# x in two column halves with the identity alone first, and the split of b_e1 behind the first residual additions, in a one-core hybrid attention and expert block

## What is computed

```python
h = rmsnorm(x, g_mix);  z = h @ w_in                     # 1024 x 5184, in column chunks
o_a, o_b = nsa_mixer(...), dsa_mixer(...)                # two sparse attentions
merged = sigmoid(ga) * (o_a @ w_branch_a) + sigmoid(gb) * (o_b @ w_branch_b)
x = x + merged @ w_out                                   # the first residual addition
x = x + moe_ffn(rmsnorm(x, g_ffn), w_router, b_router, w_e1, b_e1, w_e2, b_e2)
x = x + sigmoid(rmsnorm(x, g_ple) @ w_ple_gate) * (p @ w_ple)

# moe_ffn: the top 4 of 32 experts by router logits; for each chosen (token, expert):
gu = xe @ w1[e] + b1[e]
act = (clip(gu[:, F:], -7, 7) + 1) * min(gu[:, :F], 7) * sigmoid(1.702 * min(gu[:, :F], 7))
y += weight * (act @ w2[e] + b2[e])
```

## Time and profile before

| | us |
|---|---|
| median of 3 runs (lowest, highest) | 1254.29 (1253.6, 1255.81) |
| the profiled execution, its time | 1253.69 |
| its span in the profile | 1251.6 |
| TensorE busy | 1147.2 (92%) |
| VectorE busy | 273.8 (22%) |
| ScalarE busy | 188.6 (15%) |
| DMA queue of SyncE | 441.45 MB, 85.0% of 16 engines' span |
| chain that ended last | PE 58%, DMA 38%, ACT 2%, DVE 1% |

### The profile page before, as it was taken

One profiled execution on the slowest core, in us unless ns is written; L12 is line 12 of the kernel. 1 busy time (PEld: TensorE's weight loads), 2 busy tenths in 40 slices (PEclk: granted clock), 3 DMA queues, 4 the chain that ended last, 5 costly groups with the idle time before them and its releaser, 6 DMA issues.

```text
span 1251.6 us, 15209 instructions
## 1 busy us (share of the span) xinstructions
PE 1147.2 (92%) x6372; PEld 477.0 (38%) x6372; DVE 273.8 (22%) x786; ACT 188.6 (15%) x405; POOL 34.8 (3%) x49
## 2 busy tenths in 40 slices
PE   7999999988999999998899888888888888888878
PEld 4455544434433334333333333333333333333334
DVE  1473534243211112111111111111111111111122
ACT  2223434222111111111110000000000000000010
POOL 2121100000000000000000000000000000000000
PEclk9999999988999999999999999999999999999999
DMA  8935050966999999999999999999999999999980
GB/s 281 321 135 187 15 135 1 398 231 261 428 426 428 429 427 428 428 429 429 424 427 428 429 428 428 428 428 429 429 430 428 428 428 427 429 429 429 427 344 34
DMA packets 51209, 448.29 MB, mean 358 GB/s; under 512 B 9265, under 2 KB 11926, under 8 KB 26502
## 3 DMA queue, kind: packets, MB, share of 16 engines
q1 hardware_dynamic: 49582, 441.45, 85.0%
q0 software_dynamic: 1264, 5.27, 1.2%
q10 hardware_dynamic: 328, 1.08, 0.3%
HBM read 446.71 MB, written 4.22 MB: 360 GB/s over the span
## 4 chain that ended last, share of the span: by engine, by line
PE 58%; DMA 38%; ACT 2%; DVE 1%; issue 0%; ACTq 0%; POOL 0%; DVEq 0%; POOLq 0%
DMA ring<-in_w_e 24%; PE ps L369 16%; DMA wbuf<-in_w_e 12%; PE ps L396 11%; PE ps L1315 7%; PE ps L1397 5%; PE ps L347 3%; PE ps L338 2%; PE ps L1514 2%; PE ps L1428 2%; PE ps L1361 2%; PE ps L1449 1%; DMA oT<-in_b_e 1%; ACT wbuf L460 1%; PE ps L386 1%; PE ps L1388 1%
## 5 line engine op out<-in xcount | busy, mean ns | idle before, releaser
L369 PE MATMUL ps<-ring,wbuf 128*64 128x512 f32 x1392 | 312.1, 595 | 35.0 <-DMA ring<-in_w_e 34.8
L369 PEld LDWEIGHTS ps<-ring,wbuf 128*64 128x64 f32 x1392 | 96.0, 136 | 238.5 <-issue 162.2
L507 DVE TENSOR_SCALAR oT<-ps 128x512 f32<-128x512 f32 x32 | 22.1, 692 | 736.2 <-PE ps L369 736.2
L369 PE MATMUL ps<-wbuf 128*64 128x512 f32 x656 | 147.8, 595 | 17.6 <-DMA wbuf<-in_w_e 17.4
L396 PE MATMUL ps<-ring,wbuf 128*64 128x512 f32 x672 | 149.5, 595 | 14.2 <-ACT wbuf L460 14.2
L456 ACT ACTIVATE oT<-oT 128x512 f32<-128x512 f32 x32 | 20.2, 630 | 509.8 <-DVE oT L507 509.8
L369 PEld LDWEIGHTS ps<-wbuf 128*64 128x64 f32 x656 | 45.2, 136 | 113.4 <-issue 75.4
L1315 PE MATMUL ps<-wbuf,hT 128*128 128x512 f32 (+2 forms) x224 | 85.4, 540 | 1.0 <-ACT hT L705 1.0
L396 PE MATMUL ps<-wbuf 128*64 128x512 f32 x352 | 78.6, 595 | 7.4 <-ACT wbuf L460 7.4
L396 PEld LDWEIGHTS ps<-ring,wbuf 128*64 128x64 f32 x672 | 46.4, 137 | 102.1 <-issue 83.9
L347 PE MATMUL ps<-wbuf 64*128 64x512 f32 x264 | 65.6, 615 | 0.7 <-ACT wbuf L462 0.7
(11 more groups left out here) (237 smaller groups left out, 763.1 us busy)
## 6 DMA issues: line engine op xcount, KB each, us to landing
ring<-in_w_e SPq DMA_DIRECT2D x129, 2048.0 KB, 38.0
wbuf<-in_w_e SPq DMA_DIRECT2D x63, 2048.0 KB, 38.0
wbuf<-in_w_in SPq DMA_DIRECT2D x9, 2048.0 KB, 8.8
wbuf<-in_w_out SPq DMA_DIRECT2D x1, 4096.0 KB, 14.2
rel_rows_repeated<-rel_rows POOLq DMA_DIRECT2D x1, 3072.0 KB, 19.6
ring<-rel_rows_repeated POOLq DMA_DIRECT2D x1, 2048.0 KB, 12.7
wbuf<-in_w_branch_a SPq DMA_DIRECT2D x2, 1024.0 KB, 9.9
wbuf<-in_w_branch_b SPq DMA_DIRECT2D x1, 2048.0 KB, 16.4
```

The lines of the kernel that those rows point to most:

```text
L369: l = mm((G, Lb)[n // 2][(n % 2) * SLOTS:(n % 2 + 1) * SLOTS, :], xeT[:, k, :], slots[at][:, r * 2 * DFF + n * 512:r * 2 * DFF + (n + 1) * ...
L507: d.tensor_scalar(gc, ps[0][:, :], LIMIT, None, ALU.min).then_inc(s["gc_ready"], 1)
```

## The change

Head of the program: x is loaded in two column halves with a semaphore each. ScalarE's queue loads only the identity ahead of the gains; the other 417 columns of the constants follow in SyncE's queue behind the second chunk of `w_in`, with a semaphore of their own. Transposes X0 and X1 wait for the first half, X2 and X3 for the second. Z0 waits for the evacuations of the transposes step by step. The cast of `tri_ones` moves from the start to behind the merging on VectorE.

Before the experts: the first cast of b_e1 and the first subtraction go behind `square(1)`, the second subtraction behind `square(2)`; `add(2)` and `square(2)` come before the last parts. On ScalarE the two casts of b_e1 go behind `hi(0)` and behind `x_copy(2)`.

```diff
-                sp.dma_start(x[:, :, :], io["x"][0].rearrange("(t p) d -> p t d", p=P)).then_inc(ld_x, 16)
+                x_in = io["x"][0].rearrange("(t p) d -> p t d", p=P)
+                sp.dma_start(x[:, :, 0:512], x_in[:, :, 0:512]).then_inc(ld_x, 16)
+                sp.dma_start(x[:, :, 512:DM], x_in[:, :, 512:DM]).then_inc(ld_xb, 16)
...
                     if c == 1:
-                        sp.wait_ge(ld_x, 16)
+                        sp.wait_ge(ld_xb, 16)
...
                         sp.dma_start(onehot, io["onehot"]).then_inc(ld_tab, 16)
+                        sp.dma_start(const_all[:, P:545], io["consts"][:, P:545]).then_inc(ld_consts, 16)
...
-                sc.dma_start(const_all, cst).then_inc(ld_const, 16)
+                sc.dma_start(ident, cst[:, 0:P]).then_inc(ld_const, 16)
...
-                for i, rows in enumerate((slice(0, 2 * NE), slice(NE, 2 * NE))):
+
+                def b1_part(i, rows):
                     sc.wait_ge(b1_sub, i + 2)
                     a.copy(b1p[rows], b1f[rows]).then_inc(b1_cast, 1)
...
                 hi(0)
+                b1_part(0, slice(0, 2 * NE))
                 mid(0)
                 x_copy(2)
+                b1_part(1, slice(NE, 2 * NE))
...
                 ve.wait_ge(ld_x, 16)
+                ve.wait_ge(ld_xb, 16)
...
-                ve.wait_ge(ld_const, 16 * 4)
-                d.tensor_copy(tri_ones.rearrange("p a t -> p (a t)"), const_all[:, P:3 * P])
...
-                ve.wait_ge(ld_b1, 48)
-                d.tensor_copy(b1p, b1f).then_inc(b1_sub, 1)
-                ve.wait_ge(b1_sub, 1)
+                ve.wait_ge(ld_consts, 16)
+                d.tensor_copy(tri_ones.rearrange("p a t -> p (a t)"), const_all[:, P:3 * P])
+                def b1_first():
+                    ve.wait_ge(ld_b1, 48)
+                    d.tensor_copy(b1p, b1f).then_inc(b1_sub, 1)
+                    ve.wait_ge(b1_sub, 1)
...
-                b1_rest(0, slice(0, 2 * NE))
...
                 add(0)
                 square(0)
-                b1_rest(1, slice(NE, 2 * NE))
                 add(1)
                 square(1)
+                b1_first()
+                b1_rest(0, slice(0, 2 * NE))
                 remainder(0, 0)
                 remainder(0, 1)
+                add(2)
+                square(2)
+                b1_rest(1, slice(NE, 2 * NE))
                 last_part(0, 0)
                 last_part(0, 1)
-                add(2)
-                square(2)
...
-                        te.wait_ge(ld_x, 16)
+                        te.wait_ge(ld_x if t < 2 else ld_xb, 16)
...
-                        te.wait_ge(t_ev, 5)
...
                             for k in range(KT):
+                                if c == 0 and t == 0 and k % 2 == 0:
+                                    te.wait_ge(t_ev, 2 + k // 2)
```

More of the change, by code:

```diff
@@ L247, in block_kernel @@
         er_rep = nc.dram_tensor("rel_rows_repeated", [16, P, ERW], F32).ap()
-        ld_const, ld_x, ld_small, ld_tab, ld_ck = sem("ld_const"), sem("ld_x"), sem("ld_small"), sem("ld_tab"), sem("ld_ck")
+        ld_const, ld_consts, ld_x, ld_xb, ld_small, ld_tab, ld_ck = (sem(n) for n in ("ld_const", "ld_consts", "ld_x", "ld_xb", "ld_small", "ld_tab", "ld_ck"))
         ld_w = [sem(f"ld_w{i}") for i in range(4)]
```

## The result

| us | before | changed |
|---|---|---|
| median (lowest, highest) of 6 runs | 1254.51 (1253.4, 1257.96) | 1244.76 (1243.63, 1246.38) |
| profiled execution: time | 1253.69 | 1244.73 |
| its span | 1251.6 | 1242.8 |

The ratio is 0.9921, with a 95% interval of 0.9907 to 0.9935: faster by 9.8 us, 8 to 12. 1244.5 was forecast, so the number was met. The two traces show that one of its two terms, the part before the experts, was met for its reason, and that the other, the start, was met by luck.

What follows compares the result with a forecast made beforehand. The prediction took TensorE to bound the kernel nearly everywhere up to 298.70 us, then the experts' weights by DMA. Start 2.2 plus before the experts 7.6 gives 9.8 us off the 1254.29 median: 1244.5, range 1241.5 to 1248.5.

Steps and rivals of the forecast that it cites:

- g_ffn and half of x land 1.7 us earlier: Kernel start: fewer bytes ahead of the first loads let the transposes of x start 1.7 us earlier, bounds 0 and 1.9.
- the lower bound of 0: Kernel start: the low end for the transposes' move, 0 us, if g_ffn lands as late as before.
- The prediction's own sign for a mis-sized start: Kernel start: Z0 waiting for its weights or at half pace for more than 1 us would show the forecast wrong.
- Z0's stepwise wait, 1.03 us: Kernel start: Z0 may start at 11.42 instead of 12.45, not waiting for all four evacuations; gain 1.03 us.
- The clock gives back 0.5: Kernel start: about 1.0 us of Z0 falls before the clock's rise, at half pace, and costs 0.5 us.
- Sum of the start, 2.2: Kernel start: 1.03 + 1.7 - 0.5 = 2.2 us gained, bounds 0.5 and 3.1.
- Before the experts, 7.64: Before the experts: the last addition starts 7.64 us earlier, from 5.00 of standstill and 2.64 at the lower clock.
- b_e1 may land 4.4 us later: Before the experts: b_e1 may land up to 268.9, 4.4 us later than in the trace, before it costs anything.
- Each microsecond beyond costs one: Before the experts: from a b_e1 landing at 268.9, each microsecond later costs one.
- The experts' start moves the end one for one: Experts: bound by their weights' DMA, whose stream waits for freed buffers, so an earlier start shortens the kernel equally.
- Bounds of 5.0 and 8.6: Before the experts: 5.0 us if the clock falls in another gap, 8.6 if the stretch from 292 us regains 1.
- The estimate of 3.1 us for the start: Kernel start: by the page's fit Z0 would wait only for its weights, gaining 3.1 us instead of 2.2.

Runs made afterwards that it cites:

- start alone: Only the edits of the start, on the kernel before, with b_e1 left as before: 1253.46 us against 1255.46, ratio 0.9982.

## Why the prediction was right, and where not

The steps in their order:

- *g_ffn and half of x land 1.7 us earlier*: wrong. 7.01 us instead of 6.93. The step took the nearest queue's bytes for the cause, although showed x at work in the other at the same time; the lower bound of 0 was the true one. In the runs the loads are worth 0.0 us (1244.77 without them). The prediction's own sign for a mis-sized start came true: Z0 took 9.10 us, 1.13 more than the 7.97 at full pace, an estimated 2.3 us of it at half pace.
- *Z0's stepwise wait, 1.03 us*: right for Z0's start (0.9 earlier), too small in the medians (1.6 to 2.0). *The clock gives back 0.5*: in the pair of traces it gave back all of the 0.9. What the medians gained shows in the executions whose clock holds at the two gaps of the attention, which the prediction had no term for.
- *Sum of the start, 2.2*: met (2.0 alone) by luck, through two errors of opposite sign: 1.7 us for loads that gave nothing, and nothing for the 1.8 us that the clock can take in the attention.
- *Before the experts, 7.64*: right, 7.71 in the traces, 8.1 in the medians of the edit alone. The queues came out as worked through: nobody on TensorE waited for add(2) or for a cast.
- *b_e1 may land 4.4 us later*: right (3.36 us of standstill at 7.8 us of delay). *Each microsecond beyond costs one*: wrong, about two in the one profile (6.5 us for 3.36), through the clock.
- *The experts' start moves the end one for one*: right; the span is shorter by 8.8, the second visit starts 8.84 earlier.
- *Bounds of 5.0 and 8.6*: the 0.50 between 284 and 290 us stayed, and cost 0.7 us more this time.
- The estimate of 3.1 us for the start by the Trainium skill ("DMA: Bandwidth & Descriptors", section "Anatomy of one DMA", 2.0 us plus the bytes at 436 GB/s, fitted on GpSimd's path) fared no better. The traces of these ScalarE transfers don't agree with it: g_ffn's 4 KB took 4.84 us beside x, and 1.40, less than the fit's 2.0, without it.

VectorE's queue in the changed kernel's timeline shows this: the cast of b_e1, the first subtraction, then add(2) with what it waited for.

```profile
263.81 1.22 DVE L1123 CAST gat<-oT 96x2048 bf16<-96x2048 f32 x1
...
265.06 2.28 DVE L1129 TENSOR_TENSOR oT<-oT,gat 64x2048 f32<-64x2048 f32 x1
...
270.14 0.69 DVE L1137 TENSOR_TENSOR xres<-ps,xres 128x512 f32<-128x512 f32 x1 [1.47 <-PE ps L1460]
```

The cast follows the square at once, so b_e1 had landed by then, and add(2) waited 1.47 us for TensorE, not TensorE for it.

## To carry to other kernels

A wait at the head of an in-order queue is best moved behind everything that doesn't need it; the gain is the standstill plus what the clock loses behind it, here 5.0 + 2.6 us. Check the slack of the new place by its own chain, and price a miss above its own length where the granted clock falls behind it (here 6.5 us for 3.4). Small loads that gated the start here suffered from bulk traffic in another queue, and reordering their own queue didn't help. A single profile can't tell an edit's microsecond or two where the clock differs by as much from execution to execution; the mean granted clock of every execution can, if profiles of both kinds say which stretch each value stands for.

## What the runs showed of the hardware

- A transfer of 4 KB took 4.53 to 5.03 us to land beside 1 MB of x and a chunk of w_in in another queue (eleven profiles), and 1.40 us with no such traffic (one). x's first half, issued 2.75 us later, let the transposes start only 0.07 us later.
- The last of three transfers of b_e1 (256 KB each) landed 13.7 and 14.9 us after issue when issued right behind the seventh expert piece (kernel before, start alone), and 14.1 us when issued 7 us later.
- With the same instructions and the same waits (1.30 and 0.45 us near 108, 2.17 us near 163), TensorE's clock fell to half behind them in some executions and not in others: from the end of Z0 to the gates it is 199.4 or 197.6 us. In one profile it fell at 116 us instead, and the same stretch took 200.9. By the mean granted clock, no execution of 11 with one wait before Z0 kept its clock at both gaps, and 12 of 19 with the stepwise wait did. At the start the granted clock reads 1.00 although transposes run at half pace (1.06 us for four, 0.47 later), so there the pace tells the level and that row doesn't.
